# Two prompt tiles in the first group, two and the streams in the second

## What is computed

```python
def layer(x, c, ssd_h0, ssd_buf, lru_h0, lru_buf, ...):
    mod = (jax.nn.silu(c) @ w_mod + b_mod)[:, None, :]
    sh1, sc1, g1, sh2, sc2, g2 = jnp.split(mod, 6, axis=-1)
    h = rmsnorm(x, ln1_w) * (1.0 + sc1) + sh1
    tm, ssd_h, ssd_b, lru_h, lru_b = token_mixer(h, ssd_h0, ssd_buf, lru_h0, lru_buf, ...)
    x = x + g1 * tm
    h = rmsnorm(x, ln2_w) * (1.0 + sc2) + sh2
    x = x + g2 * peer(h, peer_wq, peer_k1, peer_k2, peer_u, peer_v)
...
def peer(h, wq, k1, k2, u, v):
    # v1, i1 = top 16 of 128 keys by each half of the query; sv, si = top 16 of the 256 sums;
    # e = the experts so found, g = softmax(sv)
    act = jax.nn.gelu(jnp.einsum('td,tkd->tk', hx, u[ex])) * gx
    return jnp.einsum('tk,tkd->td', act, v[ex])
```

## Time and profile before

| | |
|---|---|
| time, median of 3 runs | 4792.32 us (4789.23 to 4794.84) |
| the profiled execution's own time | 4792.62 us |
| its span | 4790.9 us |
| PE, DVE, ACT, POOL busy | 3664.5, 3047.8, 1133.9, 1436.0 us |
| moved by DMA | 1609.11 MB, mean 336 GB/s |
| of it by the gathers (q0) | 1342.26 MB |
| TensorE clock granted, mean | 0.87 |

### The profile page before, as it was taken

How to read it: one execution, slowest core, us unless ns; L and a number is a source line. 1 busy time by engine, 2 the same in 40 slices (tenths; PEclk the granted TensorE clock), 3 DMA queues, 4 the chain that set the end, 5 groups by cost and what they waited for, 6 DMA issues and landing times. The chain is left out here.

```text
span 4790.9 us, 53957 instructions
## 1 busy us (share of the span) xinstructions
PE 3664.5 (76%) x19330; PEld 1810.3 (38%) x19330; DVE 3047.8 (64%) x8043; ACT 1133.9 (24%) x3117; POOL 1436.0 (30%) x1298
## 2 busy tenths in 40 slices
PE   7899976777688775789999866778788775565555
PEld 4455542434354442334445422344344432111111
DVE  2443169976954577696833796956964587685554
ACT  2132022232421222232511221322411222121111
POOL 0000023323333333222322323334233333444443
PEclk9999988888899987789999987989899887777777
DMA  8333369989999999778998978999999998999997
GB/s 321 147 129 108 97 238 346 369 322 365 347 417 399 406 374 363 290 273 320 356 342 318 349 286 354 371 351 389 364 419 419 388 373 349 402 412 421 405 421 314
DMA packets 270361, 1609.11 MB, mean 336 GB/s; under 512 B 46939, under 2 KB 51857, under 8 KB 103053
## 3 DMA queue, kind: packets, MB, share of 16 engines
q0 software_dynamic: 184320, 1342.26, 70.5%
q1 hardware_dynamic: 65808, 255.49, 14.2%
q10 hardware_dynamic: 19964, 7.91, 0.6%
HBM read 1597.63 MB, written 7.91 MB: 335 GB/s over the span
## 5 line engine op out<-in xcount | busy, mean ns | idle before, releaser
L465 POOL DMA_INDIRECT ring<-in_peer_uv,eidx x1280 | 1432.8, 1119 | 3315.8 <-PE psum L858 2495.5
L858 PE MATMUL psum<-ring,diag 64*64 64x512 f32 x10240 | 1567.6, 740 | 954.1 <-ACT diag L1177 895.1
L1717 DVE SCALAR_TENSOR_TENSOR ring<-ring,hrow 128x1024 f32<-128x1024 f32 x1280 | 1546.2, 1224 | 1015.3 <-DMA ring<-in_peer_uv,eidx 1008.4
L478 PE MATMUL psum<-hT,wslot 128*128 128x384 f32 (+1 forms) x4224 | 1240.8, 449 | 5.7 <-DMA wslot<-in_w_tiles 5.7
L858 PEld LDWEIGHTS psum<-ring,diag 64*64 64x64 f32 x10240 | 388.6, 156 | 1904.2 <-ACT diag L1177 1313.4
L478 PEld LDWEIGHTS psum<-hT,wslot 128*128 128x128 f32 x4224 | 813.9, 197 | 516.1 <-issue 196.5
L1197 ACT ACTIVATE gel<-hid 128x2 f32<-128x2 f32 x640 | 129.6, 202 | 2399.3 <-DVE ring L1717 2397.7
L478 PE MATMUL psum<-region,wslot 128*128 128x384 f32 (+1 forms) x1536 | 442.1, 442 | 2.1 <-DVE region L1550 1.3
L1177 ACT ACTIVATE diag<-ident,wgt 128x64 f32<-128x64 f32 x1280 | 365.9, 333 | 0.3 <-issue 0.2
L478 PEld LDWEIGHTS psum<-region,wslot 128*128 128x128 f32 x1536 | 291.9, 194 | 174.5 <-issue 53.7
L1717 DVE DVE_READ_ACCUMULATOR ring<-ring,hrow 128x1 f32 x1280 | 105.9, 83 | 0.0
(11 more groups left out here) (253 smaller groups left out, 2806.4 us busy)
## 6 DMA issues: line engine op xcount, KB each, us to landing
wslot<-in_w_tiles SPq DMA_DIRECT2D x360, 512.0 KB, 6.3
ring<-in_w_modt SPq DMA_DIRECT2D x24, 2048.0 KB, 9.0
ring<-in_peer_uv,eidx POOLq DMA_INDIRECT x1280, 9.3
wslot<-in_w_gate SPq DMA_DIRECT2D x32, 128.0 KB, 5.0
region<-in_states_t SPq DMA_DIRECT2D x16, 256.0 KB, 13.5
region<-in_states_n SPq DMA_DIRECT2D x16, 256.0 KB, 7.9
out_new_ssd_sample<-region ACTq DMA_DIRECT2D x16, 256.0 KB, 14.0
xT<-in_x_t SPq DMA_DIRECT2D x1, 2560.0 KB, 9.3
```

The lines of the kernel that those rows point to most:

```text
L465: pool.indirect_dma_start(ring[:, n, :], None, table, bass.IndirectOffsetOnAxis(ap=eidx[:, s % 3, k:k + 1], axis=0))\
L478: last = pe.matmul(out, wslot[:, n % SLOTS, k * P:(k + 1) * P], src(k), start=k == 0, stop=k == KT - 1)
L858: last = pe.matmul(psum[c * H:(c + 1) * H, q, :], diag[rows, n, :], ring[rows, n, D + c * 512:D + (c + 1) * 512], start=k == 0, stop=k == ...
L1717: dve.scalar_tensor_tensor(out=ring[:, n, 0:D], in0=ring[:, n, 0:D], scalar=1.0, in1=hrow[:, s % 2, :], op0=ALU.mult, op1=ALU.mult, accum_ ...
```

## The change

The first group of each layer becomes tiles 0 and 1 (256 columns), the second tiles 2 and 3 with the streams (384 columns). `plan()` gets other windows: region 1 beside the pairs of tiles 0 and 1, region 2 beside tiles 2 to 4, region 3 beside tiles 5 and 6; tiles 7, 8 and 9 go with the final norms. By this plan the picks spread under the regions 1, 2 and 3 are 192, 342 and 230. The S stage has 13 steps in the first group and 22 in the second.

Since the second group is wider, its buffers are laid out anew in the same room: the incoming states have two slots, those of the update three (`state_slot`), where both shared five. A load for the products waits for the product two before it, one for the update waits for the store three before it (the first of them: for `yoff` and `dec`). The products are made in four steps of two, everything behind them in the streams' tile a step later. The tails' rows have three places, and from the fourth piece on ACT waits until the earlier ones are written; the first waits for the recurrence's end. Slices that had 128 as the prompt's part have `lay.PN`.

```diff
@@ -30,10 +30,10 @@
 TILES_E = DEPTH * NT
 
 
-FIRST, COUNT = (0, 3), (3, 2)
-T0 = (0, 3 * P)
-NG = (3 * P, 2 * P)
-PN = (3 * P, P)
+FIRST, COUNT = (0, 2), (2, 3)
+T0 = (0, 2 * P)
+NG = (2 * P, 3 * P)
+PN = (2 * P, 2 * P)
 REGIONS = 2 * DEPTH
 
 
@@ -52,7 +52,7 @@
 def bases(g):
     b = {"N1": 0, "X": 12}
     b["S"] = b["X"] + 13
-    b["Z"] = b["S"] + (19 if g == 0 else 15)
+    b["Z"] = b["S"] + (6 * COUNT[0] + 1 if g == 0 else 6 * COUNT[1] + 4)
     b["LX"] = b["Z"] + 8
     b["LRU"] = b["LX"] + 9
     b["M"] = b["LRU"] + 8
@@ -109,11 +109,12 @@
     def steps_of(r):
         return [(r, i) for i in range(LENGTH[r])]
 
-    window(fresh + pairs_of(1, 2), steps_of(1), 0, 64 - 28 + 125)
-    window(pairs_of(3, 4), steps_of(2), 9, 122)
-    window(pairs_of(5, 6, 7), steps_of(3), 9, 180)
-    window(pairs_of(8), [(REGIONS + t, i) for t in range(3) for i in range(FINAL)], 9, 60)
-    window(pairs_of(9), [(REGIONS + 3, i) for i in range(FINAL)], 9, 60)
+    window(fresh + pairs_of(1), steps_of(1), 0, 64 - 28 + 60)
+    window(pairs_of(2, 3, 4), steps_of(2), 9, 180)
+    window(pairs_of(5, 6), steps_of(3), 9, 124)
+    window(pairs_of(7), [(REGIONS + t, i) for t in range(2) for i in range(FINAL)], 9, 60)
+    for t in (2, 3):
+        window(pairs_of(6 + t), [(REGIONS + t, i) for i in range(FINAL)], 9, 60)
     for p in range(9):
         out.append(((TILES_E, p), []))
     for i in range(FINAL):
@@ -154,7 +155,7 @@
 
 def same_group(s):
 
-    return s % NT not in (2, 4)
+    return s % NT not in (FIRST[1] - 1, NT - 1)
 
 
 def choice_at(s):
@@ -167,14 +168,19 @@
     return sum(1 for u in range(s + 1) if same_group(u))
 
 
+def state_slot(i):
+
+    return i % 2 if i < 8 else (i - 8) % 3
+
+
 def state_loads(l, i):
 
-    return sum(1 for u in range(DEPTH) for v in range(16) if (u, v) <= (l, i) and v % 5 == i % 5)
+    return sum(1 for u in range(DEPTH) for v in range(16) if (u, v) <= (l, i) and state_slot(v) == state_slot(i))
 
 
 def state_stores(l, j):
 
-    return sum(1 for u in range(DEPTH) for v in range(8) if (u, v) <= (l, j) and (8 + v) % 5 == (8 + j) % 5)
+    return sum(1 for u in range(DEPTH) for v in range(8) if (u, v) <= (l, j) and v % 3 == j % 3)
 
 
 def chosen(r):
...
@@ -303,15 +309,15 @@
                 self.e = room(at, HEADS, P)
                 self.bm = room(at, 2, STREAMS * NS)
                 self.dtax = room(at + 1024, HEADS, HD)
-                self.ea = room(at + 2048, KT, P)
-                self.xdt = room(at + 3072, HEADS, HD)
-                self.stout = room(at + 3584, 512)
-                self.cbm = room(at + 4096, 2, P)
-                self.btok = room(at + 4352, P)
-                self.xw = room(at + 4480, HEADS, HD)
+                self.xw = room(at + 2048, HEADS, HD)
+                self.ea = room(at + 3072, KT, P)
+                self.xdt = room(at + 4096, HEADS, HD)
+                self.cbm = room(at + 5120, 2, P)
+                self.btok = room(at + 5376, P)
+                self.stout = room(at + 1024, 512)
                 if self.sample:
-                    self.states = room(at + 5504, 5, 512)
-                    self.tail_rows = room(27 * N, 7, 512)
+                    self.states = (room(at + 5504, 512), room(at + 6016, 512), room(at + 1536, 512))
+                    self.tail_rows = room(22 * N, 3, 512)
                 self.xpad = room(10 * N, 2, self.pad + 1)
                 self.xacc = room(10 * N + 2 * (self.pad + 1), 2, self.pad + 1)
                 self.xth = room(10 * N + 4 * (self.pad + 1), 2, N)
...
@@ -374,14 +380,15 @@
 
                     lay = G[1]
                     for i in range(16):
-                        slot = i % 5
-                        if i >= 5:
-                            if i - 5 < 8:
-                                sp.wait_ge(S["yoff"], at("yoff", l, i - 5))
-                            else:
-                                sp.wait_ge(state_out[slot], 16 * state_stores(l, i - 13))
+                        slot = state_slot(i)
+                        if 2 <= i < 10:
+                            sp.wait_ge(S["yoff"], at("yoff", l, i - 2))
+                        elif i == 10:
+                            sp.wait_ge(S["dec"], l + 1)
+                        elif i > 10:
+                            sp.wait_ge(state_out[slot], 16 * state_stores(l, i - 11))
                         name = "states_t" if i < 8 else "states_n"
-                        sp.dma_start(lay.states[:, slot, :], a[name].rearrange("l i p c -> p (l i) c")[:, l * 8 + i % 8, :])\
+                        sp.dma_start(lay.states[slot], a[name].rearrange("l i p c -> p (l i) c")[:, l * 8 + i % 8, :])\
                           .then_inc(state_in[slot], 16)
 
                 for r in range(REGIONS):
...
@@ -632,17 +639,17 @@
                         stream_parts(l, lay, tt, i)
 
                 def stream_parts(l, lay, tt, i):
-                    if 5 <= i <= 7:
+                    if 5 <= i <= 8:
                         if i == 5:
                             pe.wait_ge(S["e"], at("e", tt, 3))
-                        for b in ((0, 1), (2, 3, 4), (5, 6, 7))[i - 5]:
-                            pe.wait_ge(state_in[b % 5], 16 * state_loads(l, b))
+                        for b in (2 * i - 10, 2 * i - 9):
+                            pe.wait_ge(state_in[b % 2], 16 * state_loads(l, b))
                             for j in range(8):
                                 po = 64 * (j % 2)
                                 for q in range(2):
                                     rows = slice(64 * q, 64 * q + 64)
                                     last = pe.matmul(bank(5 + q)[po:po + 64, j // 2 * P + b * SLEN:j // 2 * P + (b + 1) * SLEN],
-                                                     lay.states[rows, b % 5, j * HD:(j + 1) * HD],
+                                                     lay.states[b % 2][rows, j * HD:(j + 1) * HD],
                                                      lay.ea[rows, j, b * SLEN:(b + 1) * SLEN], start=True, stop=True)
                             last.then_inc(S["yoff"], 1)
                     if i == 7:
@@ -651,17 +658,17 @@
                             last = pe.matmul(bank(7)[:, j * 8:(j + 1) * 8], lay.dtax[:, 2 * j:2 * j + 2, :].rearrange("p h c -> p (h c)"),
                                              stream_of[:], start=True, stop=True)
                         last.then_inc(S["dec"], 1)
-                    if 9 <= i <= 12:
+                    if 10 <= i <= 13:
                         pe.wait_ge(S["bm"], l + 1)
                         pe.wait_ge(S["xw"], at("xw", tt))
-                        for j in (2 * i - 18, 2 * i - 17):
+                        for j in (2 * i - 20, 2 * i - 19):
                             if j < 2:
                                 pe.wait_ge(S["ysoff"], l + 1)
                             else:
                                 pe.wait_ge(S["sadded"], at("sadded", l, j - 2))
                             pe.matmul(bank(5 + j % 2), lay.xw[:, 2 * j:2 * j + 2, :].rearrange("p h c -> p (h c)"), lay.bm[:, j // 4, :],
                                       start=True, stop=True).then_inc(S["sadd"], 1)
-                    if i == 9:
+                    if i == 10:
                         pe.wait_ge(S["dece"], l + 1)
                         for j in range(4):
                             last = pe.transpose(bank(7)[:, j * P:(j + 1) * P], stT[:, j * P:(j + 1) * P], ident[:])
...
@@ -1010,7 +1017,7 @@
                             if l:
                                 act.wait_ge(S["sadded"], at("sadded", l - 1, 7))
                             act.activation(dece[:], bank(7)[:, 0:64], ACT.Exp).then_inc(S["dece"], 1)
-                        if i == 10:
+                        if i == 11:
                             act.wait_ge(S["stout"], l + 1)
                             act.activation(lay.stout, bank(7), ACT.Copy).then_inc(S["stcopy"], 1)
                             act.wait_ge(S["stcopy"], l + 1)
@@ -1018,11 +1025,11 @@
                             v = lay.stout.rearrange("p (j q n) -> p q j n", j=4, q=2)
                             for q in range(2):
                                 act.dma_start(out[:, l, q, :, :], v[:, q, :, :]).then_inc(written, 16)
-                        if 11 <= i <= 14:
-                            for j in (2 * i - 22, 2 * i - 21):
+                        if 12 <= i <= 15:
+                            for j in (2 * i - 24, 2 * i - 23):
                                 act.wait_ge(S["sadded"], at("sadded", l, j))
-                                act.dma_start(dst[:, l, j, :, :], lay.states[:, (8 + j) % 5, :].rearrange("p (b n) -> p b n", b=STREAMS))\
-                                   .then_inc(state_out[(8 + j) % 5], 16)
+                                act.dma_start(dst[:, l, j, :, :], lay.states[j % 3].rearrange("p (b n) -> p b n", b=STREAMS))\
+                                   .then_inc(state_out[j % 3], 16)
 
                 def ssd_stage(r, i):
```

(21 more changed lines are left out.)

48 lines of the change are left out of this document (24 added, 24 removed).

## The result

The changed kernel takes 4808.19 us (median of six runs, 4805.16 to 4817.92), the kernel before in the same comparison 4793.58 us (six runs, 4784.75 to 4805.89). The ratio is 1.0033 with a 95% interval of 1.0017 to 1.0049, so it is slower by 8 to 23 us. The prediction said slower by 68. The profiled execution took 4810.64 us, 18.0 more than that of before.

The account below looks back on a forecast made before the run. PE bounds the front and wide regions, gather loop and DMA the narrow ones and tail. 496 + 161 + 941 + 1054 + 986 + 212 + 979 + 30 = 4859 us, forecast 4860; range 4780 to 4965.

Parts of the forecast that it names:

- Front: Before the first gathered product: 256 instead of 384 columns saves 157 us (120 to 185), moving it from 653 to 496.
- First stretch: The 56 picks after the front, 182 us before: seven heads with one search less each save 21 us, giving 161.
- PE's share in wide regions: Regions 1 and 3 after: PE work of 808 and 848 us at region 2's share 0.893 gives 905 and 950 us.
- (a): Incoming states, SSD stage: three load rounds in a row, about 8.5 us idle each, 26 instead of about 10: +16 us.
- Rival 2: Wide regions: better-fed PE rises from 0.89 to 0.95 share; sum 4675 us, 4767 with half of that; chance 0.13.
- Its new waits: State round trips through fewer slots in regions 1 and 3: 36 us each, bounds 0 and 75; region 1 941 us.
- (b): Update, Z stage: loads wait for stores, round trip 21.9 us; idle 10, 3 and 12 us, less 5 before: +20.
- rival 1: The states' round trips hide, both wide regions lose their 36 us; sum 4787 us, no change; chance 0.07.
- Region 2: After, 256 columns, no streams, 342 picks: region 3 before (1089 us) without the streams, 1054 us, between 1020 and 1089.
- Gaps, tail and end: Gaps 212 us for 76 picks; tail with a third tile 979 us; the last 30 us stay.

Follow-up runs that it names:

- the kernel without those loads: Changed kernel with six of each layer's eight incoming-state loads left out, the update's loads and stores kept: 4790.98 us, ratio 0.9989 to the kernel before.
- the halved kernels: Changed kernel and kernel before, each with half of every projection's products left out: 4515.38 us (0.9424) and 4513.72 us (0.9417).
- the first run on picks: Changed kernel with region 1's steps spread over 80 pairs instead of 96, moving 32 picks to the gap behind: 4858.02 us, ratio 1.0130.
- the kernel with four places: Changed kernel with four slots for incoming states instead of two, the update's first two loads also starting two products earlier: 4795.41 us, ratio 1.0013.
- the slots alone: Kernel before, old grouping kept, with only the changed slot scheme (two incoming, three for the update): 4800.7 us, ratio 1.0027.

## Why the prediction was right in sign and wrong in size

**Front: right.** The first gathered rows are used at 497.5 for 496. In the front's merge stage the tiles start 3.5 us apart, as 16 x 0.217, and ACT's cycle in the gates, which sets the distance of the first two rows here, is 6.06 us:
```profile
307.46 3.72 PE L485 MATMUL psum<-hT,wslot 128*128 128x256 f32 x16 [0.99 <-ACT region L1088]
313.53 3.72 PE L485 MATMUL psum<-region,wslot 128*128 128x256 f32 x16 [2.34 <-ACT region L1088]
317.08 3.62 PE L485 MATMUL psum<-hT,wslot 128*128 128x256 f32 x16
320.54 3.62 PE L485 MATMUL psum<-region,wslot 128*128 128x256 f32 x16
```

**First stretch: 15 us too low.** I took 3 us off each head for the missing search. DVE's work fell by 16 us (163.15 to 147.07), but the stretch only by 6.7 us for seven heads, one each. POOL's timeline shows gathers of the stretch waiting for PE to release the ring, up to 9.75 us at a time; this is the first such wait.
```profile
510.23 0.93 POOL L472 DMA_INDIRECT ring<-in_peer_uv,eidx  x1 [8.25 <-PE psum L865]
```
My reading is that the loop through the ring (gather, dot on DVE, values, product, release) sets the pace of a head, and a search is only partly in it. That DVE was busy for 163 of 182 us was not enough to call it the bound. No run takes this apart, so the reading stays unproven.

**PE's share in wide regions: right in number, with a narrower cause.** Without the waits of (a) region 1 is 898.7 us, where 905 stood, and region 3 is 951.4, where 950 stood. PE's work after is 803.42 and 839.27 us (808 and 848), and in the kernel without those loads PE is busy for 0.89 and 0.88 of the two regions (0.893). But the halved kernels show that 0.89 is a mixture: merge is at 1.00 and hangs on PE, while query and SSD don't move with PE's work. That the share could be carried over because region 1 after has the stages and the width of region 2 before is argued, not tested. Rival 2 expected fewer picks to raise the share to 0.95; with 32 picks less (the first run on picks) it was 776.78 of 871, still 0.89.

**Its new waits: the step that failed.** The 36 us a layer, terms (a) and (b), were mis-sized: the regions show 8.3 and 19.7 us for (a), and for (b) PE's own waits show no more than before.
- (a) Going in. I priced each round at a landing of 13.5 us, less a step of 4.7: 26 us a layer, of which 10 old. Leaving all six late loads of a layer out gains 8.3 us in region 1 and 19.7 in region 3. PE's own idle times before these products are 6.75 us at most, against 4.75 before, and their sum didn't rise at all (20.6 us in six waits before, 18.5 in six after):
```profile
874.71 1.05 PE L651 MATMUL psum<-region 64*64 64x16 f32 x32 [4.80 <-DMA region<-in_states_t]
...
3020.57 1.91 PE L651 MATMUL psum<-region 64*64 64x16 f32 x64 [6.75 <-DMA region<-in_states_t]
```
- (b) The update. I took 20 us a layer, from a round trip of 21.9 us. DVE does wait, as foreseen, for up to 9.37 us:
```profile
3065.42 0.69 DVE L1460 TENSOR_TENSOR region<-region,dece_t 128x512 f32<-128x512 f32 x1 [9.37 <-DMA region<-in_states_n]
```
In region 1's Z stage DVE has only 38.90 us of work in 60, and PE has 55.73: most of the wait falls into DVE's slack. PE's waits for the update's sums are 2 us in region 1 and 7.7 in region 3, 9.6 in all, and they were 9.9 before. I had named what is queued behind the wait, but not asked whether that engine was the late one there.

A second slip pulls the other way. I took off 10 and 5 us a layer as old waits, but the base of 0.893 comes from region 2, which has no streams and so none of them. By its own logic the sum should have been 30 us higher, and further off.

The landing of 13.5 us for (a) came mostly from loads issued in bunches beside the gathers of a narrow region, as shown above. The landings of the changed kernel's own loads aren't in its profile; in the kernel with four places the same loads took 2.5 to 8.9 us, also where four were issued within 2 us. The stores got faster too, the page's line and the line's own view in after:
```profile
out_new_ssd_sample<-region ACTq DMA_DIRECT2D x16, 256.0 KB, 8.0
...
DMA to landing us min/median/max: 2.6/8.0/18.3
```
against a median of 14.0 and a slowest of 30.3 before (the landings of only six of the sixteen are known after). With the slots alone they took 8.7, the slowest 42.8. I counted store and load at 21.9 us together; 8.0 and the 6.7 of the load in the kernel with the slots alone make 14.7. The Trainium skill ("DMA: Bandwidth & Descriptors", section "🔬 Anatomy of one DMA — SWDGE (gpsimd) path") has a fixed 2 us plus the bytes at 436 GB/s, for transfers that GpSimd issues; the estimate of 2.6 us for 256 KB is worked out from that. The fastest store of after, which ACT issued, took 2.6 us and the median three times that, so here the estimate is about the least that a landing takes and not the usual.

The result lies nearer to rival 1, which gave back all of the 72 us and so some 20 too many. Its reason, landings "in the thin DMA moments of PE-bound stretches", agrees with the two loads of region 1 that took 4.1 us in the new grouping and 12.2 in the old. In region 3 the pair was faster too, at a DMA share of 0.98. With 8.3 and 19.7 us for the two layers in place of 36 each, the sum is 4859 - 44 = 4815, and the rest (first stretch +15, region 2 -12, the remainder of regions 1 and 3 at -5, front, gaps, tail and end -4) nearly cancels, to 4809.

**Region 2: 12 us too high.** Without the streams it is 47 us shorter than region 3 before (1089 to 1042.1), where I took 35. The whole stretch now runs at 3.05 us a pick with the DMA share at 0.97.

**Gaps, tail and end: right.** 208, 981 and 26 us for 212, 979 and 30. (Of the 212, 4 us were a slip: 213 us for 78 picks make 207.5 for 76.) Three tiles at 2.55 us a pick, at a DMA share of 0.99 to 1.00, are what makes the change a loss. The front and first stretch save 162 us, the regions 140, the gaps and the end 8, and the tail takes 328: the difference is the 18 us of the profiled executions. With four places for the incoming states it is a draw. The 128 picks more in the tail cost 328 us, and front, first stretch and regions together save 302.
